# Expert selection started one query group earlier and reordered by halves, later picks, and masked sums in four column tiles

## What is computed

```python
q = (xt @ w_query).reshape(T, PEER_HEADS, 2, PEER_HALF)        # 256 tokens, 8 heads, 2 halves
scores = jnp.einsum('thpc,hpnc->thpn', q, sub_keys)            # 128 keys a half
vals, idx = lax.top_k(scores, 16)
cand = (vals[..., 0, :, None] + vals[..., 1, None, :])         # 16 x 16 sums a head
top_vals, top_c = lax.top_k(cand, 16)
experts = i1 * 128 + i2                                        # 128 experts a token
gates = softmax(top_vals)
hdn = gelu(einsum('ted,td->te', expert_down[experts], xt))
y   = einsum('te,ted->td', gates * hdn, expert_up[experts])
```

## Time and profile before

| | us |
|---|---|
| median of 3 runs | 2964.51 |
| lowest, highest | 2962.3, 2968.74 |
| the profiled execution | 2959.61 |
| its span, first to last instruction | 2957.8 |

### The profile page before, as it was taken

How to read it: one execution, slowest core, us unless ns; L and a number is a source line. 1 busy time by engine, 2 the same in 40 slices (tenths; PEclk the granted TensorE clock), 3 DMA queues, 4 the chain that set the end, 5 groups by cost and what they waited for, 6 DMA issues and landing times.

```text
span 2957.8 us, 41368 instructions
## 1 busy us (share of the span) xinstructions
PE 2832.6 (96%) x16385; PEld 2343.4 (79%) x16385; DVE 2064.4 (70%) x3109; ACT 1118.0 (38%) x1741; POOL 553.0 (19%) x534
## 2 busy tenths in 40 slices
PE   5799999999999999899999999999999989999997
PEld 4699999997879988798887799888898978444443
DVE  5778777778775456744656668985668999566666
ACT  3344444445454445644455541112036986000000
POOL 1000000000000000000000002234345458545443
PEclk9999999999999999999999999999999999999999
DMA  9987787877866634365443546999988888999997
GB/s 385 351 267 265 265 266 265 266 264 260 299 207 179 175 111 167 125 203 175 138 127 119 192 155 235 319 340 404 406 325 285 294 304 313 405 410 409 409 410 320
DMA packets 345761, 799.60 MB, mean 270 GB/s; under 512 B 40105, under 2 KB 95649, under 8 KB 344801
## 3 DMA queue, kind: packets, MB, share of 16 engines
q1 hardware_dynamic: 270576, 505.70, 50.0%
q0 software_dynamic: 74992, 291.27, 26.4%
HBM read 794.76 MB, written 2.10 MB: 269 GB/s over the span
## 4 chain that ended last, share of the span: by engine, by line
PE 65%; DMA 16%; DVE 6%; ACT 5%; POOL 4%; issue 4%; SPq 0%; DVEq 0%; ACTq 0%; POOLq 0%
PE ps L2020 16%; PE ps L2022 15%; PE ps L2021 15%; PE ps L2582 13%; DMA s<-in_up_rows,s 12%; POOL s L714 4%; DMA s<-in_down_rows,s 2%; DMA s<-in_ada_first 2%; DVE s L1973 1%; ACT s L1161 1%; DVE r L1244 1%; DVE s L1954 1%; DMA s<-in_ret_first 1%; ACT r L729 1%; PE ps L2314 1%
## 5 line engine op out<-in xcount | busy, mean ns | idle before, releaser
L2020 PE MATMUL ps<-r,r 128*128 128x256 f32 (+1 forms) x3232 | 1042.4, 323 | 9.8 <-DVE r L1244 7.5
L2022 PE MATMUL ps<-r,r 128*128 128x256 f32 (+1 forms) x3232 | 1023.8, 317 | 0.0
L2021 PE MATMUL ps<-r,r 128*128 128x256 f32 (+1 forms) x3232 | 1023.3, 317 | 0.0
L1244 DVE TENSOR_TENSOR r<-s,r 128x1024 fp32r<-128x1024 f32 (+2 forms) x532 | 640.2, 1212 | 425.5 <-ACT r L729 424.4
L729 ACT CAST r<-s 128x1024 fp32r<-128x1024 f32 (+2 forms) x532 | 548.9, 1039 | 765.8 <-PE ps L2022 706.1
L2020 PEld LDWEIGHTS ps<-r,r 128*128 128x128 f32 x3232 | 617.3, 191 | 66.0 <-issue 19.8
L2021 PEld LDWEIGHTS ps<-r,r 128*128 128x128 f32 x3232 | 617.5, 191 | 42.6 <-issue 5.3
L2022 PEld LDWEIGHTS ps<-r,r 128*128 128x128 f32 x3232 | 616.9, 191 | 39.8
L2708 PE MATMUL ps<-s,big 128*128 128x512 f32 x1024 | 442.5, 595 | 1.3 <-DMA s<-in_up_blocks 1.3
L1973 DVE SCALAR_TENSOR_TENSOR s<-s,s,s 128x1024 f32<-128x1024 f32 x256 | 328.6, 1284 | 163.8 <-DMA s<-in_up_rows,s 162.3
L1954 DVE CUSTOM_DVE_ANT_0 s<-s,s 128x1152 f32<-128x1152 f32 x256 | 345.5, 1353 | 107.6 <-DMA s<-in_down_rows,s 107.2
(11 more groups left out here) (314 smaller groups left out, 2328.0 us busy)
## 6 DMA issues: line engine op xcount, KB each, us to landing
s<-in_ada_w SPq DMA_DIRECT2D x128, 512.0 KB, 5.3
s<-in_up_blocks SPq DMA_DIRECT2D x128, 512.0 KB, 6.8
s<-in_ret_w_in SPq DMA_DIRECT2D x112, 512.0 KB, 5.4
s<-in_down_blocks SPq DMA_DIRECT2D x128, 448.0 KB, 6.5
s<-in_w_in SPq DMA_DIRECT2D x96, 512.0 KB, 3.9
s<-in_ada_first SPq DMA_DIRECT2D x64, 512.0 KB, 7.9
s<-in_ret_w_out SPq DMA_DIRECT2D x64, 512.0 KB, 5.7
s<-in_ret_w_in SPq DMA_DIRECT2D x112, 256.0 KB, 3.9
```

What stands on the lines that cost most here:

```text
L1244: v.tensor_tensor(lo_of(w), raw_of(w), hi_of(w).bitcast(F), ALU.subtract).then_inc(*lo_made.to(w))
L2020: pe.matmul(o, lh, rh, start=start, stop=False, skip_group_check=True)
L2021: pe.matmul(o, lh, rl, start=False, stop=False, skip_group_check=True)
L2022: return pe.matmul(o, ll, rh, start=False, stop=stop, skip_group_check=True)
```

## The change

Four things are changed; all line numbers in the text are those of the kernel before.

- The score blocks of groups 0 to 2 are made and copied inside the query stage, behind units 1 and 3 of the next group; only the two blocks of group 3 stand behind the last unit.
- `select(t, f)` does one half, and the halves run in the order (0,0), (1,0), (0,1), (1,1). `gate_in` is made in two halves, so there are 296 steps. From unit 10 on 4 steps follow every unit (88 steps in the stage), and 4 go in front of every row.
- Picks begin after row 150 instead of 139 and stand closer (6/5 of a row instead of 7/5); those of tile 1 begin after row 189 instead of 185; the coefficient steps move from 190 to 194. PE turns the picks of tile 0 at block pair 24 instead of 20.
- Four tokens of a pick are now q, 32 + q, 64 + q, 96 + q, and each of the four matmuls of `add_picked` writes only its own 32 rows of SUMS, with a 32-column window.

```diff
-        WINDOW = at(144 * KB + 1536, 255)
+        WINDOW = at(144 * KB + 1536, 63)
+        def token(q, k):
+            return 32 * k + q
...
-        PICK_AT = [139 + 7 * q // 5 for q in range(32)] + [185 + 2 * q for q in range(32)]
-        HOT_AT = [190 + 2 * q for q in range(29)] + [248, 250, 251]
+        PICK_AT = [150 + 6 * q // 5 for q in range(32)] + [189 + 2 * q for q in range(32)]
+        HOT_AT = [194 + 2 * q for q in range(29)] + [251, 252, 253]
...
-                    if g == 2 and u == 1:
-                        sel_copy(0, 0)
-                        sel_copy(0, 1)
+                    if g and u in (1, 3):
+                        sel_copy(u // 2, g - 1)
...
-                if q in (20, 40):
-                    picks(q // 20 - 1)
+                if q in (24, 40):
+                    picks(q // 40)
...
             def both():
-                for t in range(2):
-                    yield from select(t)
+                for f in range(2):
+                    for t in range(2):
+                        yield from select(t, f)
             choice = both()
-            left = 73
             for g in range(4):
                 for u in range(8):
                     step(PQW + 8 * g + u)
-                    if g >= 2 and u % 2:
-                        for _ in range(8):
-                            if left:
-                                next(choice)
-                                left -= 1
-            while left:
-                next(choice)
-                left -= 1
+                    if 8 * g + u >= 10:
+                        for _ in range(4):
+                            next(choice)
...
-                    for _ in range(5):
+                    for _ in range(4):
                         next(choice, None)
...
-                if n == 186:
+                if n == 190:
                     hidden(0)
-                if n == 188:
+                if n == 192:
                     coefficients(0)
...
-                    if g == 2 and u == 1:
-                        sel_scores(0, 0)
-                        sel_scores(0, 1)
+                    if g and u in (1, 3):
+                        sel_scores(u // 2, g - 1)
...
             for t in range(2):
-                for g in range(4):
-                    if (t, g) not in ((0, 0), (0, 1)):
-                        sel_scores(t, g)
+                sel_scores(t, 3)
...
-                    n = 4 * q + k
-                    r = pe.matmul(SUMS, WINDOW[:, 127 - n:255 - n], PR[(32 * t + q) % 3][:, k * 128:(k + 1) * 128],
-                                  start=n == 0, stop=n == 127, skip_group_check=True)
+                    r = pe.matmul(SUMS[32 * k:32 * k + 32, :], WINDOW[:, 31 - q:63 - q], PR[(32 * t + q) % 3][:, k * 128:(k + 1) * 128],
+                                  start=q == 0, stop=q == 31, skip_group_check=True)
```

More of the change, by code:

```diff
@@ L1848, in select @@
                     yield
-                    for h in range(4 * f, 4 * f + 4):
-                        v.wait_ge(*steps.at())
-                        yield from top16(CA[:, h % 4, :], TV[:, h, :], TC[:, h * 16:(h + 1) * 16].bitcast(U32), WK)
-                    s6 = slice(64 * f, 64 * f + 64)
                     v.wait_ge(*steps.at())
-                    v.tensor_scalar(II[0][:, s6].bitcast(U32), TC[:, s6].bitcast(U32), 4, None, ALU.logical_shift_right)
+                    v.tensor_tensor(E4, E4, I2[:, :, p, :].unsqueeze(2).broadcast_to([128, 4, 16, 16]),
+                                    ALU.mult).then_inc(*steps.to())
@@ L1874, in select @@
-                    v.wait_ge(*steps.at())
-                    v.scalar_tensor_tensor(out=EI[t][:, s6].bitcast(U32), in0=EF[t][:, 0, s6], scalar=128.0,
-                                           in1=EF[t][:, 1, s6],
-                                           op0=ALU.mult, op1=ALU.add).then_inc(*chosen.to((t, f)))
-                    v.wait_ge(*chosen.at((t, f)))
-                    yield
-                v.tensor_tensor(GT[t], TV, TV[:, :, 0:1].broadcast_to([128, 8, 16]), ALU.subtract).then_inc(*gate_in.to(t))
+                v.wait_ge(*steps.at())
@@ L1881, in select @@
+                if f:
+                    r.then_inc(*gate_in.to(t))
                 yield
@@ L1918, in pick @@
                     v.wait_ge(*steps.at())
-                    v.memset(WINDOW[:, 127:128], 1.0).then_inc(*steps.to())
+                    v.memset(WINDOW[:, 31:32], 1.0).then_inc(*steps.to())
                     v.wait_ge(*steps.at())
@@ L2594, in spread_ @@
                 for k in range(4):
-                    r = pe.matmul(bank[b][:, k * 128:(k + 1) * 128], IDR[:, 4 * q + k:4 * q + k + 1].broadcast_to([128, 128]),
+                    r = pe.matmul(bank[b][:, k * 128:(k + 1) * 128], IDR[:, token(q, k):token(q, k) + 1].broadcast_to([128, 128]),
                                   EFR[t][:, 1, :], start=True, stop=True)
@@ L2612, in pick_rows @@
                 for k in range(4):
-                    pe.matmul(bank[b][:, k * 128:(k + 1) * 128], DH[:, 128 * t + 4 * q + k, :], PH[q % 2][:, k, :],
+                    pe.matmul(bank[b][:, k * 128:(k + 1) * 128], DH[:, 128 * t + token(q, k), :], PH[q % 2][:, k, :],
                               start=True, stop=True)
@@ L2616, in pick_rows @@
                 for k in range(4):
-                    r = pe.matmul(bank[b1][:, k * 128:(k + 1) * 128], IDR[:, 4 * q + k:4 * q + k + 1].broadcast_to([128, 128]),
+                    r = pe.matmul(bank[b1][:, k * 128:(k + 1) * 128], IDR[:, token(q, k):token(q, k) + 1].broadcast_to([128, 128]),
                                   EFR[t][:, 0, :], start=True, stop=True)
```

81 lines of the change are left out of this document (45 added, 36 removed).

## The result

| | before | changed | ratio, 95% interval |
|---|---|---|---|
| median of 5 runs each | 2966.37 us | 2948.63 us | 0.9942 [0.9931, 0.9953] |
| lowest, highest | 2962.3, 2970.67 | 2945.62, 2950.64 | |
| medians of 11 and 6 more runs | 2964.35 | 2949.64 | 0.9942 [0.993, 0.9955] |

The second ratio sets the changed kernel's six runs against 23 runs of the kernel before that were taken beside them (median 2965.86).
The change brings 17.7 us by the first pair of medians (forecast 19.9). The profiled execution of the changed kernel took 2950.64 us, its span is 2948.8.

What follows compares the result with a forecast made beforehand. Two chains, PE's and the rows', run side by side and meet three times. Terms +3.6 - 17.2 - 6.0 - 0.3 = -19.9 take the profiled 2959.6 to 2939.7; the median's 4.9 more gives 2944.6 us, range 2936 to 2958.

Steps and rivals of the forecast that it cites:

- Query stage: Score blocks and more selection inside it: dense blocks 2.0 us later, first row 7 us earlier, PE cost 0, at worst 3.
- The stall of block 2: Early dense part: block 2 is loaded with gathers in flight, 1.5 us of stall, 0 to 3.
- Rows up to the picks: Before the first pick: row 56 waits for `gate_in(1)`, rows are 17 us ahead from there, row 150 done at 2192.
- the rows are not there: Rival: row 56's wait eats the shorter portions' gain; total -14 or -9, 2950 to 2956 us; chance 0.10.
- Picks of tile 0: First pick to tile 1's first pick: 39 rows instead of 46, 77 us instead of 94.3, so -17.2.
- the third limit: Tile 0's picks: four row buffers, each taken 7.95 us, give 1.99 us a row, 77.5 us for 39; the highest limit.
- PE's share: Tile 0's picks on PE: masked sums 0.45 instead of 0.86 us, 2.27 instead of 2.68 a pick, 73 us for 32.
- Picks of tile 1: ACT is full at 4.08 us a pick and two rows a pick stay two: change 0.
- Up to `hidden(1)`: From 2413.3: four rows instead of eight, 10.6 us instead of 16.6, so -6.0 (-3 to -8).
- the signs of being wrong: PE idle between query-stage units, first pick after 2200, tile 0's picks still 2.7 us, or granted clock below 0.95 in them.
- Column tiles gain nothing: Rival: switching form leaves tile 0's picks at 2.68 us of PE, total about -9, 2956 us; chance 0.11.
- The clock: Rival: PE gaps in tile 0's picks bring 1.2 GHz; ten slow picks lose 20 us; chance 0.06, shared with other large costs.

Runs made afterwards that it cites:

- late_blocks: Changed kernel with the first dense up-block loaded when pick (1,4) is done, not when the last down-block is: ratio to before 0.9948.
- early60: Changed kernel with the selection's scratch free for rows from row 60, not 56: ratio to before 0.9947.
- hybrid: Changed kernel with column tiles for tile 0's picks only, tile 1's masked sums 128 columns wide again: 2950.6 us, ratio to before 0.9948.
- picks146: Changed kernel with tile 0's picks behind rows 146 + 4q/3 instead of 150 + 6q/5: 2956.29 us, ratio to before 0.9966.
- combined: Changed kernel with edits of early60, late_blocks and hybrid, picks at 153 + 8q/7 and 190 + 2q, coefficient steps later: 2947.39 us, ratio to before 0.9937.

## Why the prediction was right, step by step

- **Query stage, right.** PE lost nothing, DVE had the room (66.5 us of work in 89). Dense blocks +1.8 and +1.9 us (said 2.0); first gather at 1801.3 with the whole stage 1.8 us later in this trace, so 1799.5 (said 1799.7); first row 8 us earlier (said 7). The stall of block 2 was 0.8, said 1.5. The dense part ended 2.9 and 3.0 us later than before, said 3.6.
- **Rows up to the picks, right with one exception.** POOL waited for `gate_in(1)` as foretold, and row 56 came 16 and 19 us earlier (said 17). The rival "the rows are not there" is half seen: in the first trace row 150 kept PE waiting for 5.4 us. The second trace, `late_blocks` and `early60` had it in time, and the time was the same: of the 5.3 us between the first picks of the two traces, 1.8 came back in tile 0's picks, 1.4 in tile 1's and the rest behind them.
- **Picks of tile 0: mechanism right, size off.** The step that failed is the third limit, "Buffers: ... 7.95 / 4 = 1.99 a row, 77.5 us for 39". It named the right limit, as far as DVE's waits and the sum of 8.28 us above show it; in the changed kernel's two traces a row costs 2.07 and 2.12, so 81 to 83 us and -13 instead of -17.2. The sum of issue, median landing and row left out that a landed row waits for DVE (0.24 us on average), and the forecast took the higher of two limits, where DVE's own 72.4 and 72.8 us (said 72.5) and its waits for rows add up. The same stretch of the kernel before had the number in it: 94.3 us for 46 rows are 2.05, and 39 of those are 80.
- **PE's share, right.** 2.29 us a pick (said 2.27), when nothing holds it up; the whole stretch has 2.53 and 2.58 us a pick, said 2.4. The Trainium skill ("TensorEngine Tiling (Array Packing)", Key Properties) has TensorE drained at a change of tiling mode. By the rows, going in costs 0.57 us from the matmul before (2212.37 to 2212.94) against 0.48 (2263.12 to 2263.60) in the kernel without column tiles, so 0.09, and the four sums with the way out take 0.36, together the 0.45 of the forecast. If the drain is there, going in it takes 0.09 us at most, and 0.41 of the 0.86 us are saved all the same.
- **Picks of tile 1: said 0, came out +1 to +2.5.** 1.2 us of it is the order: the last pick now stands behind a coefficient step (DVE, 2411.98) that waits 0.52 us for PE, and follows the one before it by 5.0 us instead of 3.8, in both traces of each. The other 1.3 us of the second trace lie behind the first six picks of the tile, at the full clock: the next 24 take 98.2 us instead of 96.9. Their cause is open. The lower level at the start of the stage is a smaller matter: with 13.7 to 17.1 us of it (`hybrid`, `late_blocks`, `early60`, column tiles alone) the first six picks take 26.6 to 27.2 us, in both kernels' traces 25.4 to 25.7.
- **Up to `hidden(1)`, right.** -7.2 and -6.7, said -6.0.
- **Sum.** In the second traces +3.0 for the first pick, -12.9, +2.5 and -6.7 make -14.1, and the spans differ by 15.5; the rest lies in the out-projection's end (+0.3), in the dense up part (-0.1) and behind it (-1.6). These two traces are 1.9 and 1.1 us above their medians. The first traces differ by only 9.0, since that of before was 4.9 us under its median of the time (6.8 under that of five runs) and that of the changed kernel 2.0 above. The medians differ by 17.7 and 14.7. The forecast's -19.9 had 4 too much in the picks of tile 0 and nothing for tile 1.
- **Rivals, and the signs of being wrong.** Column tiles gain nothing: true in the kernel before; with 39 rows they shorten the stretch by 2.6 to 4.4 us. The clock: in both traces falls to 0.50 did come among tile 0's picks, 6.8 and 3.4 us in the first and 3.4 twice in the second, the last time just ahead of the change of tiles. With them 0.94 was granted in that stretch of the first trace, below the 0.95 that the prediction had named as a sign. The first pick came after 2200 in both (2204.31 and 2200.27), another such sign. Neither cost what was feared. Counted from the out-projection's end the second trace's first pick is at 507.6, 1 us behind the forecast, and the first trace, with both signs at their strongest, has the shorter picks of tile 0 (80.8 against 82.6) and the same span. Its first low stretch follows the 5.38 us in which PE waited:

```profile
2204.50:2211.00 6.50, 5.89 (x37) 4.88 (x37) 5.71 (x9) 2.44 (x4) 3.17 (x4) 0.50 0.81 249
```

## What to carry to other kernels

Where two chains meet at fixed points of an instruction list, a lead won by one is worth nothing until the meeting point is moved too: the earlier selection alone and the later picks alone both cost 0.1%, together they brought 0.5%. To size such a move, count what stands between two meeting points and multiply by the pace that the same stretch shows in the trace, not by a pace put together from single durations. And read idle time on both sides of a meeting point. With the selection alone DVE stood for 19.67 and 3.94 us, about 10 rows at 2.33 us: an estimate of how far the point has to move, and the change moves it by 11. Seven rows (`picks146`) gave 0.9966, eleven 0.9942, fourteen (`combined`, with other edits in it) 0.9937.
